# Last unit of expert rows in a hybrid attention block: six of sixteen rows added on VectorE, eight buffers, other PSUM banks, and a closing norm by quarters

## What is computed

```python
a = jax.nn.gelu(jnp.einsum('bchkd,bcd->bchk', U[e], xc), approximate=False)
return jnp.einsum('bchk,bchkd->bcd', g * a, V[e])
...
h = h + peer_ffn(rms_norm(h, norm_ffn_g[l]), ...)
return rms_norm(h, norm_final_g)
```

## Time and profile before

| | us |
|---|---|
| median of 3 runs | 2355.86 |
| lowest, highest | 2353.65, 2356.53 |
| profiled execution, span from first to last instruction | 2357.4 |
| busy: TensorE, VectorE, ScalarE, GpSimd | 1949.4, 1371.5, 623.4, 706.6 |
| mean rate of the DMA over the span | 297 GB/s |

### The profile page before, as it was taken

How to read it: one execution, slowest core, us unless ns; L and a number is a source line. 1 busy time by engine, 2 the same in 40 slices (tenths; PEclk the granted TensorE clock), 3 DMA queues, 4 the chain that set the end, 5 groups by cost and what they waited for, 6 DMA issues and landing times.

```text
span 2357.4 us, 23487 instructions
## 1 busy us (share of the span) xinstructions
PE 1949.4 (83%) x6815; PEld 1181.7 (50%) x6815; DVE 1371.5 (58%) x2206; ACT 623.4 (26%) x1093; POOL 706.6 (30%) x600
## 2 busy tenths in 40 slices
PE   5999999999999988787777777777777777777777
PEld 4788787777778766674222322222332223222233
DVE  5445556776756554677566556655665666566531
ACT  4444444555444344341111111111011111101111
POOL 0000000000000000015555455455645554555421
PEclk9999999999989999899999999999999999999999
DMA  6566743434345653389999999999999999999996
GB/s 230 161 193 191 217 137 97 113 110 116 107 124 180 226 176 109 117 317 360 421 418 415 423 416 418 420 422 421 421 422 422 418 422 422 421 422 422 422 389 234
DMA packets 158728, 700.73 MB, mean 297 GB/s; under 512 B 16352, under 2 KB 20832, under 8 KB 91488
## 3 DMA queue, kind: packets, MB, share of 16 engines
q0 software_dynamic: 73728, 536.90, 55.3%
q1 hardware_dynamic: 83280, 162.94, 22.3%
q10 hardware_dynamic: 1680, 0.41, 0.1%
HBM read 698.11 MB, written 2.10 MB: 297 GB/s over the span
## 4 chain that ended last, share of the span: by engine, by line
PE 43%; DMA 35%; issue 10%; DVE 7%; ACT 2%; POOL 1%; SPq 0%; ACTq 0%; DVEq 0%; POOLq 0%
DMA v_ring<-in_peer_v_dram,idx_v 17%; DMA big<-in_peer_u_dram,idx_u 16%; PE banks L541 10%; PE banks L543 9%; PE banks L542 9%; PE banks L880 7%; PE banks L527 2%; PE banks L626 2%; PE banks L645 2%; DVE big L1657 1%; DMA wraw<-in_peer_wq_dram 1%; DVE ws L1284 1%; ACT ws L926 1%; PE banks L636 1%; DMA wraw<-in_w_out_dram 1%
## 5 line engine op out<-in xcount | busy, mean ns | idle before, releaser
L880 PE MATMUL banks<-v_ring,kxT 128*128 128x512 f32 x2048 | 957.0, 613 | 307.9 <-DMA v_ring<-in_peer_v_dram,idx_v 268.1
L880 PEld LDWEIGHTS banks<-v_ring,kxT 128*128 128x128 f32 x2048 | 376.6, 193 | 887.6 <-issue 652.6
L1657 DVE SCALAR_TENSOR_TENSOR big<-big,xn 128x2048 f32<-128x2048 f32 x256 | 586.7, 2292 | 401.0 <-DMA big<-in_peer_u_dram,idx_u 398.1
L1284 DVE TENSOR_TENSOR ws<-wraw,ws 128x1024 fp32r<-128x1024 f32 (+1 forms) x288 | 345.1, 1204 | 266.0 <-ACT ws L926 263.1
L485 POOL DMA_INDIRECT big<-in_peer_u_dram,idx_u x256 | 366.6, 1432 | 352.3 <-DVE big L1657 128.9
L490 POOL DMA_INDIRECT v_ring<-in_peer_v_dram,idx_v x256 | 301.4, 1177 | 359.2 <-PE banks L880 313.8
L926 ACT ACTIVATE ws<-wraw 128x1024 fp32r<-128x1024 f32 (+1 forms) x288 | 296.7, 1035 | 319.3 <-PE banks L543 273.1
L541 PE MATMUL banks<-ws,xr 128*128 128x512 f32 x896 | 361.4, 403 | 15.8 <-DVE ws L1284 9.5
L542 PE MATMUL banks<-ws,xr 128*128 128x512 f32 x896 | 352.8, 394 | 0.0
L543 PE MATMUL banks<-ws,xr 128*128 128x512 f32 x896 | 352.7, 394 | 0.0
L1211 ACT ACTIVATE kxT<-ident,ga 128x128 f32<-128x128 f32 x256 | 94.4, 396 | 673.5 <-PE banks L880 668.5
(11 more groups left out here) (214 smaller groups left out, 1324.0 us busy)
## 6 DMA issues: line engine op xcount, KB each, us to landing
wraw<-in_w_in_dram SPq DMA_DIRECT2D x152, 512.0 KB, 3.6
wraw<-in_w_out_dram SPq DMA_DIRECT2D x32, 512.0 KB, 4.0
wraw<-in_peer_wq_dram SPq DMA_DIRECT2D x32, 512.0 KB, 4.6
wraw<-in_w_xkv_dram SPq DMA_DIRECT2D x16, 512.0 KB, 4.8
wraw<-in_w_branch_da_dram SPq DMA_DIRECT2D x16, 512.0 KB, 3.8
wraw<-in_w_branch_nsa_dram SPq DMA_DIRECT2D x16, 512.0 KB, 3.7
wraw<-in_w_xq_dram SPq DMA_DIRECT2D x8, 512.0 KB, 4.0
wraw<-in_w_xo_dram SPq DMA_DIRECT2D x8, 512.0 KB, 3.6
```

Of the source, the lines that this page charges most:

```text
L880: last = nc.tensor.matmul(B[4 + n], diag[:, r, :], v_ring[:, r, n * NW:(n + 1) * NW], start=(j == 0), stop=(j == PK - 1))
L1284: V.tensor_tensor(ws[:, q % WR, 1, :, 0:cols], wraw[:, q % WR, :, 0:cols], ws[:, q % WR, 0, :, 0:cols].bitcast(F32), ALU.subtract).then_in ...
L1657: V.scalar_tensor_tensor(out=product, in0=u_ring[:, r, :], scalar=1.0, in1=xn3[:, par, :], op0=ALU.mult, op1=ALU.mult, accum_out=dots[:, p ...
```

## The change

Only the last unit (u = 15, tile 1) and the last norm differ.

- The 16 V gathers of the last unit alternate between v_ring (even slots) and u_ring (odd slots), four buffers of each, so eight in turn (last_slot). The first four odd ones wait for dot_done of the last four dots; later ones wait until the slot that used the buffer before has been consumed, by TensorE (v_used) or by VectorE (v_added).
- Slots 1, 4, 7, 10, 13 and 15 are multiplied by their column of ga and added to h[:, 1, :] by one VectorE instruction each (add_slot). The ten others go through TensorE with diagonals as before, into banks 0 to 3; TensorE does not wait for the sum of unit 14.
- VectorE's order is: sum of unit 14 into tile 0, slots 1 and 4, mean square of tile 0, slot 7, scaling of tile 0, slots 10, 13, 15, then the four banks to h by quarters of 512 columns.
- ScalarE squares tile 1 by quarters; the mean is formed from three partial sums and then the fourth; GpSimd's power follows; VectorE scales by quarters, and SyncE writes tile 1 in four DMAs of 256 KB.

```diff
@@ -97,6 +97,8 @@
 
 LAG = 2
 RING = 4
+ADD_SLOTS = (1, 4, 7, 10, 13, 15)
+MUL_SLOTS = tuple(j for j in range(PK) if j not in ADD_SLOTS)
 
 BIG = C * QKV_COLS + C * 2 * D
 RES_KB = 157
@@ -241,6 +243,7 @@
         rec = sb("rec", [P, 8])
         coef = sb("coef", [P, 4])
         tmp3 = sb("tmp3", [P, 3 * N_DK])
+        last_ssq, last_msq = tmp3[:, 0:4], tmp3[:, 4:8]
         cs = sb("cs", [P, C, 2, N_CMP])
         cmx = sb("cmx", [P, 4])
         csum = sb("csum", [P, 4])
@@ -310,6 +313,21 @@
         dot_done, v_used, route_scores, route_exp, gelu_done, ga_ready, diag_ready, vacc_free, y_done = map(
             sem, ("dot_done", "v_used", "route_scores", "route_exp", "gelu_done", "ga_ready", "diag_ready", "vacc_free", "y_done"))
 
+        h_last = sem("h_last")
+        v_added, last_sq, last_ms, last_rstd = map(sem, ("v_added", "last_sq", "last_ms", "last_rstd"))
+
+        def last_slot(j):
+
+            return (v_ring, u_ring)[j % 2][:, j % (2 * RING) // 2, :]
+
+        def last_landed(eng, j):
+
+            r, turn = j % (2 * RING) // 2, j // (2 * RING) + 1
+            if j % 2 == 0:
+                eng.wait_ge(v_landed[r], (UNITS - 1) * 64 + 16 * turn)
+            else:
+                eng.wait_ge(u_landed[r], UNITS * 64 + 16 * turn)
+
         x_v = x[0].rearrange("(c p) d -> p c d", p=P)
         mem_v = mem[0].rearrange("(c p) d -> p c d", p=P)
         out_v = out[0].rearrange("(c p) d -> p c d", p=P)
@@ -399,10 +417,12 @@
                     load(n, i + T_PQ, pq[n][:, :, bass.ds(i * NW, NW)])
             sp.wait_ge(w_split, N_TILES * PIECES + WR)
             sp.dma_start(gfin[:, :], norm_final_g.partition_broadcast(P)).then_inc(gfin_landed, 16)
-            for c in range(C):
-                sp.wait_ge(y_done, c + 1)
-                sp.dma_start(out_v[:, c, :], xn3[:, c, :]).then_inc(out_landed, 16)
-            sp.wait_ge(out_landed, 16 * C)
+            sp.wait_ge(y_done, 1)
+            sp.dma_start(out_v[:, 0, :], xn3[:, 0, :]).then_inc(out_landed, 16)
+            for q in range(4):
+                sp.wait_ge(y_done, q + 2)
+                sp.dma_start(out_v[:, 1, q * NW:(q + 1) * NW], xn3[:, 1, q * NW:(q + 1) * NW]).then_inc(out_landed, 16)
+            sp.wait_ge(out_landed, 16 * 5)
 
 
         @block.gpsimd
@@ -496,9 +516,27 @@
             with pool.Fori(0, PH - 1) as i:
                 step(0, True, True, i * 2 + 2)
                 step(1, True, True, i * 2 + 3)
-            step(0, False, True, UNITS)
+
+            pool.wait_ge(v_used, UNITS * 16 + (RING - 32))
+            nc.gpsimd.tensor_copy(idx_v[1][:, :], idx_u[1][:, :]).then_inc(idx_v_ready, 1)
+            pool.wait_ge(idx_v_ready, UNITS)
+            for j in range(PK):
+                k, r = j - 2 * RING, j % (2 * RING) // 2
+                if k < 0:
+                    if j % 2 == 0:
+                        pool.wait_ge(v_used, (UNITS - 1) * 16 + r + 1)
+                    else:
+                        pool.wait_ge(dot_done, UNITS * 16 + r + 1)
+                elif k in MUL_SLOTS:
+                    pool.wait_ge(v_used, (UNITS - 1) * 16 + RING + MUL_SLOTS.index(k) + 1)
+                else:
+                    pool.wait_ge(v_added, ADD_SLOTS.index(k) + 1)
+                nc.gpsimd.indirect_dma_start(last_slot(j), None, peer_v[0],
+                                             bass.IndirectOffsetOnAxis(ap=idx_v[1][:, j:j + 1], axis=0)
+                                             ).then_inc((v_landed, u_landed)[j % 2][r], 16)
             rsqrt(4, 0)
-            rsqrt(5, 0)
+            pool.wait_ge(last_ms, 1)
+            nc.gpsimd.tensor_tensor(rstd[:, 10:11], msq[:, 10:11], nhalf[:, 0:1], ALU.pow).then_inc(last_rstd, 1)
 
 
         @block.tensor
@@ -881,8 +919,19 @@
                                                 start=(j == 0), stop=(j == PK - 1))
                     last.then_inc(v_used, 1)
 
-            with pe.Fori(0, UNITS) as i:
+            with pe.Fori(0, UNITS - 1) as i:
                 v_step(i)
+
+            for c in range(C):
+                pe.wait_ge(acc_free[c], A_PQ + N_PQ + 1)
+                pe.wait_ge(tp_free[c], (G_PQ + 14) // 2 + 2)
+            for p, j in enumerate(MUL_SLOTS):
+                last_landed(pe, j)
+                pe.wait_ge(diag_ready, (UNITS - 1) * 16 + (p + 1))
+                for n in range(4):
+                    last = nc.tensor.matmul(B[n], diag[:, p % RING, :], last_slot(j)[:, n * NW:(n + 1) * NW],
+                                            start=(p == 0), stop=(p == len(MUL_SLOTS) - 1))
+                last.then_inc(v_used, 1)
 
 
         @block.scalar
@@ -1223,12 +1272,19 @@
             diagonals(0, UNITS - 2, range(PK))
             gelu(1, UNITS - 1)
             act.wait_ge(ga_ready, UNITS)
-            diagonals(1, UNITS - 1, range(0, 4))
+
+            def last_diagonals(ps):
+                for p in ps:
+                    act.wait_ge(v_used, (UNITS - 1) * 16 + (p + 1))
+                    A(diag[:, p % RING, :], ident[:, :], ACT.Copy, scale=ga[:, 1, MUL_SLOTS[p]:MUL_SLOTS[p] + 1]).then_inc(diag_ready, 1)
+
+            last_diagonals(range(0, 5))
             act.wait_ge(vacc_free, UNITS)
-            squares(12, ssq[:, 8:9], h[:, 0, :], u_ring[:, 0, :])
-            diagonals(1, UNITS - 1, range(4, PK))
-            act.wait_ge(vacc_free, UNITS + 1)
-            squares(13, ssq[:, 10:11], h[:, 1, :], u_ring[:, 0, :])
+            squares(12, ssq[:, 8:9], h[:, 0, :], product)
+            last_diagonals(range(5, len(MUL_SLOTS)))
+            for q in range(4):
+                act.wait_ge(h_last, q + 1)
+                A(product[:, q * NW:(q + 1) * NW], h[:, 1, q * NW:(q + 1) * NW], ACT.Square, accum_out=last_ssq[:, q:q + 1]).then_inc(last_sq, 1)
 
 
         @block.vector
@@ -1723,13 +1779,44 @@
             weigh(UNITS - 1, 1)
 
 
+
+            def add_slot(j):
+
+                last_landed(dve, j)
+                if j != ADD_SLOTS[0]:
+                    dve.wait_ge(v_added, ADD_SLOTS.index(j))
+                V.scalar_tensor_tensor(out=h[:, 1, :], in0=last_slot(j), scalar=ga[:, 1, j:j + 1], in1=h[:, 1, :],
+                                       op0=ALU.mult, op1=ALU.add).then_inc(v_added, 1)
+
+            dve.wait_ge(vacc_free, UNITS - 1)
+            dve.wait_ge(ga_ready, UNITS)
+            add_out(UNITS - 2, 0)
+            for j in ADD_SLOTS[0:2]:
+                add_slot(j)
+            mean_square(4, 0, 13)
+            for j in ADD_SLOTS[2:3]:
+                add_slot(j)
             dve.wait_ge(gfin_landed, 16)
-            for c in range(C):
-                add_out(UNITS - 2 + c, c)
-                n = 4 + c
-                mean_square(n, 0, 13 + c)
-                dve.wait_ge(rstd_done, norm_count(n, 0))
-                V.scalar_tensor_tensor(out=xn3[:, c, :], in0=h[:, c, :], scalar=rstd[:, 2 * n:2 * n + 1], in1=gfin[:, :],
+            dve.wait_ge(rstd_done, norm_count(4, 0))
+            V.scalar_tensor_tensor(out=xn3[:, 0, :], in0=h[:, 0, :], scalar=rstd[:, 8:9], in1=gfin[:, :],
+                                   op0=ALU.mult, op1=ALU.mult).then_inc(y_done, 1)
+            for j in ADD_SLOTS[3:]:
+                add_slot(j)
+            dve.wait_ge(v_added, len(ADD_SLOTS))
+            dve.wait_ge(v_used, (UNITS - 1) * 16 + len(MUL_SLOTS) + RING)
+            for q in range(4):
+                cols = slice(q * NW, (q + 1) * NW)
+                V.tensor_tensor(h[:, 1, cols], B[q], h[:, 1, cols], ALU.add).then_inc(h_last, 1)
+            dve.wait_ge(last_sq, 3)
+            link(V.reduce_sum(last_msq[:, 0:1], last_ssq[:, 0:3], axis=AX.X))
+            link(V.tensor_scalar(last_msq[:, 1:2], last_msq[:, 0:1], 1.0 / D, EPS, ALU.mult, ALU.add))
+            dve.wait_ge(last_sq, 4)
+            V.scalar_tensor_tensor(out=msq[:, 10:11], in0=last_ssq[:, 3:4], scalar=1.0 / D, in1=last_msq[:, 1:2],
+                                   op0=ALU.mult, op1=ALU.add).then_inc(last_ms, 1)
+            dve.wait_ge(last_rstd, 1)
+            for q in range(4):
+                cols = slice(q * NW, (q + 1) * NW)
+                V.scalar_tensor_tensor(out=xn3[:, 1, cols], in0=h[:, 1, cols], scalar=rstd[:, 10:11], in1=gfin[:, cols],
                                        op0=ALU.mult, op1=ALU.mult).then_inc(y_done, 1)
```

## The result

| us | before | after |
|---|---|---|
| median | 2356.2 (4 runs, 2353.65 to 2357.3) | 2339.47 (4 runs, 2336.57 to 2341.03) |
| profiled execution, span | 2357.4 | 2334.7 |

The ratio is 0.9922, with a 95% interval of 0.991 to 0.9934: 16.7 us faster by the medians, against 18.9 forecast. The forecast time was 2337.0, in a range of 2333.0 to 2343.0.

What follows compares the result with a forecast made beforehand. The prediction took TensorE to bind the last unit, until the gathers bind. It summed 17.0 us from the last row's end and 1.9 from the tail to 18.9 us, giving 2337.0 us from the median, range 2333.0 to 2343.0.

Steps and rivals of the forecast that it cites:

- TensorE bound the last unit, and the gathers bind it now: Last unit: TensorE's 3.45 us a row bound it; with six rows added on VectorE, gathers land every 2.485 us.
- rival 2: Last unit's gathers stay at 3.07 us each, so row 15 lands 8.8 us later: 2345.8 us; chance 0.09.
- Issue side has slack, eight buffers: Last unit's gathers: GpSimd issues the later ones 12 to 16 us before each landing, so the queue doesn't run dry.
- the rival of held issues: The six VectorE adds each hold a GpSimd gather issue by 2.04 us, 12.2 us in all: 2349.2 us; chance 0.05.
- The write moves the last gathers by 2.54 us: Tile 0's 1 MB output, leaving with rows 11 to 15 queued, delays everything behind it by 2.54 us; bounds zero and 3.9.
- rival 1: Tile 0's write fits into gaps of the reads, so the end comes 2.54 us earlier: 2334.5 us; chance 0.12.
- Row 14 on TensorE: 3.7 us, ending 1.1 us ahead of VectorE: Last unit's end: row 14 lands at 2322.9 and ends on TensorE at 2326.6; VectorE's last add ends at 2327.7.
- a fallen clock in the last row: TensorE's last row at half speed takes 6.9 us, ending 2.1 us behind VectorE; part of a rival with chance 0.02.
- Squares at a pace of 0.83 us: Closing norm: ScalarE squares tile 1 by quarters, three paces of 0.83 us and a last square of 0.72.
- The output: 1.90 us to land and 1.3 behind it: Tile 1's last output quarter takes 1.90 us to land, 1.26 fixed plus 0.64; 1.3 us follows to the span's end.
- The large term: Saving from the last row's end in the last unit: 17.0 us of the 18.9 forecast.
- The tail's term: Saving behind the last row, from the closing norm and output by quarters: 1.9 us of the 18.9 forecast.

Runs made afterwards that it cites:

- the second execution: The changed kernel run again without any edit, set against the kernel before on the same chip: 56.7 us from mark to end, ratio 0.9924.

## Why the prediction was right

- **TensorE bound the last unit, and the gathers bind it now.** Right, and rival 2 (gathers below the steady rate) falls: 422 GB/s for 35 us, rows 0 to 11 at a pace of 2.485 us, and waiting for the sum of unit 14 changes nothing. Two adds fewer change nothing either, but bring TensorE back as the bound.
- **Issue side has slack, eight buffers.** Right; the rival of held issues did not happen. The prediction didn't price what four buffers would have cost, 6.7 us of the 16.7.
- **The write moves the last gathers by 2.54 us.** Right: 2.4 us by the means, 3.0 in the first profile, so rival 1 (the write hides) falls. But the prediction set it ahead of row 11, so that row 12 would end on TensorE at 39.4 us, with 0.3 us of idle time ahead of row 14. In fact row 11 was on time, row 12 ended at 36.9 us, and the whole delay lay ahead of row 14. The Trainium skill (DMA: Bandwidth & Descriptors, SWDGE vs HWDGE vs iDMA) says that a DMA engine takes turns between the two kinds of queue. The trace agrees: from 2310.3 to 2312.3 us each had 51.2% of the engines.
- **Row 14 on TensorE: 3.7 us, ending 1.1 us ahead of VectorE.** The first mis-sized term. TensorE stood 3.48 us in one piece and its clock fell; the row took 5.32 us and ended 0.5 us behind VectorE's last add. The closing sum started at 45.8 us instead of 44.5 (2327.7 and a wait, less 2283.2). Half of these 1.3 us is the wait for TensorE (0.64 us). The other half is the last add, which started at 42.8 for 42.2 as the last row landed later. In the second execution the add was on time and the wait 0.43 us: 45.0. The prediction had named a fallen clock in the last row (2.1 us) as a rival's part and not in the forecast.
- **Squares at a pace of 0.83 us.** Mis-sized the other way: 0.61 to 0.63, so 7.0 us in place of 7.6 to VectorE's end.
- **The output: 1.90 us to land and 1.3 behind it.** Wrong as a path, though small in the sum: 4.72 us from VectorE's end in place of 3.2. Landing (2.1 us) was about right, but neither it nor the 3.8 us of before set the end. The end is set by GpSimd's DRAIN, 8.06 us from the start of the power to the end of the span, before as after; the prediction's terms give 6.5 for this way. So the tail brought 1.0 us, from the sum and the squares ahead of the power, and not the 1.9 that the prediction put down to the output.

Together: 1.3 us at the closing sum, 0.6 back in the squares and 1.5 behind VectorE's end are 2.2 us, by which 57.5 exceeds the 55.3 of the forecast (2338.5 less 2283.2). From the last add's end to the end of the span it was 12.3 us, where the prediction wanted to see 10.8. The large term, 17.0 us up to the closing sum, was right in mechanism and came out at 15.8. The tail's term was not, and only its small size kept it from mattering.

## What to carry over

When one engine binds a stage and the DMA has room, hand rows over only until the landings bind, and count what else the DMA engines carry then: a write that was free before is on the path, and holding it back until the last gather has landed was worth another 2 to 4 us. Give the handed-over rows the buffers to keep the queue full: with four instead of eight, 6.7 of the 16.7 us were lost. Do not split the last output before a run without it has shown that it sets the end. And where a wait names an engine that had long been done, look at every engine's last records: here GpSimd's set the end.

## What was not expected of the hardware

GpSimd's DRAIN at the end of the block took 7.87 us, while those of VectorE and ScalarE took 2.8 and 0.8 us in the changed kernel; with it, 8.06 us pass between the start of GpSimd's power and the end of the span, in all thirteen profiles. TensorE's clock fell in the last row behind idle times of 3.48, 3.41, 2.90 and 2.27 us, and stayed up behind 2.45, 1.88 and 1.27 us, so the length of the idle time alone does not tell. An issue of GpSimd that met an add took up to 2.8 us in place of 0.94. The Trainium skill (SBUF — State Buffer, Who interferes with whom) says that a VectorE instruction with two inputs in SBUF contends with a GpSimd instruction that reads SBUF; the adds have two such inputs, and the issues agree.
